# Two transformer blocks on one core: the first feed-forward matrix with 512-column matmuls, weights split three slabs ahead, and another rule for choosing weight buffers

## The reference, cut to what matters

```python
D_MODEL, SEQ, DEPTH, D_FF = 1024, 256, 2, 2816

def rmsnorm(x, g):
    y = xf * lax.rsqrt(jnp.mean(xf * xf, axis=-1, keepdims=True) + NORM_EPS)
    return y * g

def swiglu(x, w_in, w_out):                    # w_in 1024 x 5632, w_out 2816 x 1024
    a, b = jnp.split(x @ w_in, 2, axis=-1)
    return (jax.nn.silu(a) * b) @ w_out

for l in range(DEPTH):                         # first block; the second has the same frame
    x = x + 0.5 * swiglu(rmsnorm(x, ffn1_norm[l]), w_ffn1_in[l], w_ffn1_out[l])
    u = rmsnorm(x, mix_norm[l])
    ...                                        # u @ w_in[l], three branches, their gates
    x = x + merged @ w_out[l]
    x = x + 0.5 * swiglu(rmsnorm(x, ffn2_norm[l]), w_ffn2_in[l], w_ffn2_out[l])
```

## Time and profile before

| | |
|---|---|
| three timed executions, median | 3184.57 us |
| the profiled execution, device time | 3180.34 us |
| its span | 3178.6 us |
| TensorE busy in it | 2964.9 us (93%), 21202 matmuls |
| VectorE busy | 1693.3 us (53%) |
| ScalarE busy | 1389.1 us (44%) |
| granted TensorE clock, mean | 0.964 of full speed |
| DMA | 476.49 MB, mean 150 GB/s |

### The profile page before, as it was taken

The page is one execution under the profiler, slowest core; times in us unless marked ns, Lnnn a source line. Parts: engine busy times, 40 slices in busy tenths (PEclk is TensorE's granted clock), DMA queues, the critical chain, the costliest instruction groups (busy, mean ns, idle before and its releaser), DMA issues.

```text
span 3178.6 us, 49355 instructions
## 1 busy us (share of the span) xinstructions
PE 2964.9 (93%) x21202; PEld 2769.7 (87%) x21202; DVE 1693.3 (53%) x2846; ACT 1389.1 (44%) x1948; POOL 12.6 (0%) x20
## 2 busy tenths in 40 slices
PE   5998989999999899999999898899999999889997
PEld 5998778899998777799899896689989999667997
DVE  6656531566665842266665334456666643444665
ACT  4435442343444544244343345444444434544443
POOL 0000000000000000000000000000000000000000
PEclk9999999999999899999999899999999999899998
DMA  6543374555554242555464652355545565234552
GB/s 197 180 159 116 97 151 137 182 184 179 186 175 151 68 133 93 174 181 179 152 210 151 169 135 80 80 146 183 179 160 186 176 171 135 79 80 140 179 188 94
DMA packets 493544, 476.49 MB, mean 150 GB/s; under 512 B 63472, under 2 KB 476688, under 8 KB 493200
## 3 DMA queue, kind: packets, MB, share of 16 engines
q1 hardware_dynamic: 489744, 462.85, 47.0%
q0 software_dynamic: 3584, 10.49, 1.6%
HBM read 467.01 MB, written 6.29 MB: 149 GB/s over the span
## 4 chain that ended last, share of the span: by engine, by line
PE 87%; DVE 5%; ACT 4%; DMA 2%; issue 1%; SPq 0%; DVEq 0%; ACTq 0%
PE ps L781 36%; PE ps L852 31%; PE ps L872 16%; PE ps L954 2%; DVE WL L1539 1%; PE ps L812 1%; PE ps L929 1%; ACT REGION L1303 1%; DMA RAW<-in_w_o_mla 1%; DMA RAW<-in_w_in 1%; DMA RAW<-in_w_branch 0%; ACT REGION L1216 0%; ACT WH L1234 0%; ACT L1303 0%; ACT L1222 0%
## 5 line engine op out<-in xcount | busy, mean ns | idle before, releaser
L1539 DVE TENSOR_TENSOR WL<-RAW,WH 128x2048 fp32r<-128x2048 f32 (+1 forms) x342 | 761.4, 2234 | 476.8 <-ACT WH L1234 475.0
L1234 ACT ACTIVATE WH<-RAW 128x2048 fp32r<-128x2048 f32 (+1 forms) x342 | 633.2, 1858 | 238.5 <-DMA RAW<-in_ffn_wo 112.3
L781 PE MATMUL ps<-REGION,RAW 128*128 128x256 f32 (+3 forms) x1904 | 406.9, 376 | 65.1 <-DMA RAW<-in_w_o_mla 19.5
L781 PEld LDWEIGHTS ps<-REGION,RAW 128*128 128x128 f32 (+2 forms) x1904 | 346.7, 195 | 124.7 <-issue 50.5
L852 PE MATMUL ps<-UH,WH 128*128 128x256 f32 x2816 | 401.7, 285 | 29.8 <-ACT WH L1234 24.2
L852 PE MATMUL ps<-UH,WL 128*128 128x256 f32 x2816 | 395.1, 284 | 9.3 <-DVE WL L1539 9.3
L872 PE MATMUL ps<-HH,WH 128*128 128x256 f32 x1408 | 395.8, 281 | 2.4 <-DVE WL L1539 2.4
L872 PE MATMUL ps<-HH,WL 128*128 128x256 f32 x1408 | 396.1, 281 | 0.0
L872 PE MATMUL ps<-HL,WH 128*128 128x256 f32 x1408 | 395.5, 281 | 0.0
L852 PE MATMUL ps<-UL,WH 128*128 128x256 f32 x2816 | 394.2, 283 | 0.0
L852 PEld LDWEIGHTS ps<-UH,WH 128*128 128x128 f32 x2816 | 364.6, 192 | 33.9 <-issue 29.1
(11 more groups left out here) (212 smaller groups left out, 3067.0 us busy)
## 6 DMA issues: line engine op xcount, KB each, us to landing
RAW<-in_w_ffn_in SPq DMA_DIRECT2D x88, 1024.0 KB, 5.1
RAW<-in_ffn_wi SPq DMA_DIRECT2D x88, 1024.0 KB, 5.1
RAW<-in_w_in SPq DMA_DIRECT2D x86, 1024.0 KB, 5.5
RAW<-in_w_ffn_out SPq DMA_DIRECT2D x32, 1024.0 KB, 5.3
RAW<-in_ffn_wo SPq DMA_DIRECT2D x32, 1024.0 KB, 5.2
RAW<-in_w_out SPq DMA_DIRECT2D x16, 1024.0 KB, 8.8
RAW<-in_w_ffn_out SPq DMA_DIRECT2D x16, 768.0 KB, 4.4
RAW<-in_ffn_wo SPq DMA_DIRECT2D x16, 768.0 KB, 4.5
```

The lines of the kernel that those rows point to most:

```text
L781: last = nc.tensor.matmul(o, a, b, start=i == 0, stop=i == len(terms) - 1)
L1234: nc.scalar.activation(part_high(s), raw[pl.place[s]][:, 0:pl.words[s]], ACT.Copy).then_inc(weights_high, 1)
L1539: v_.tensor_tensor(part_low(s), raw[pl.place[s]][:, 0:pl.words[s]], part_high(s).bitcast(FP), ALU.subtract)\
```

## The change

Four edits, all in one:

1. `UH` and `UL` become two halves of one tile `UHL`, side by side for each feature tile. From slab 1 on, a product of the first matrix takes for each k one matmul with `WH` and 512 columns (UH and UL at once) and one with `WL` and 256 columns. The result stands in two halves of the bank: columns 0 to 255 hold WH·UH + WL·UH, columns 256 to 511 hold WH·UL.
2. The halves have to be added. For 42 of the 44 products ScalarE copies the second half to `TMP[:, side, T:2T]` (new function `tails`), VectorE waits for that copy (`tail_out`), adds it to the first half, and then multiplies by `RSTD` in a second instruction that waits for the first (`link`). Before, one multiplication did it.
3. The splits of the feed-forward part stand three slabs ahead (`AHEAD = 3`) where they stood two ahead.
4. `Plan.slab` takes the place that is free first by product number (`free_at`), the end of other use of `REGION` counted in, where it took the place with the oldest slab.

```diff
+AHEAD = 3
...
+    def free_at(self, p):
+        used = -1 if self.latest[p] is None else self.slab_last[self.latest[p]]
+        idle = -1 if self.idle_from[p] is None else self.idle_from[p]
+        return max(used, idle), -1 if self.latest[p] is None else self.latest[p], p
...
-        place = min(places, key=lambda p: (-1 if self.latest[p] is None else self.latest[p], p))
+        place = min(places, key=self.free_at)
...
-        UH, UL = sb("UH", [P, DK, T], FR), sb("UL", [P, DK, T], FR)
+        UHL = sb("UHL", [P, DK, 2, T], FR)
+        UH, UL = UHL[:, :, 0, :], UHL[:, :, 1, :]
...  # TensorE, ffn
+                        if j > 0:
+                            for k in range(DK):
+                                cols = slice(side * P, (side + 1) * P)
+                                both = (wh[:, k, cols], UHL[:, k, :, :], bank(n, 0, 2 * T))
+                                tail = (wl[:, k, cols], UH[:, k, :], bank(n, 0, T))
+                                for a, b, o in (both, tail) if k < DK - 1 else (tail, both):
+                                    last = nc.tensor.matmul(o, a, b, start=k == 0 and a is both[0], stop=k == DK - 1 and a is both[0])
+                            last.then_inc(product_done, 1)
+                            continue
...  # ScalarE, ffn
+                def tails(n):
+                    for side in range(2):
+                        wait_product(act, n + side)
+                        nc.scalar.activation(TMP[:, side, T:2 * T], bank(n + side, T, 2 * T), ACT.Copy).then_inc(tail_out, 1)
-                feed.to(s0 + 1)
+                feed.to(s0 + AHEAD - 1)
                 for j in range(FK // 2):
-                    feed.to(s0 + 2 * j + 2)
+                    feed.to(s0 + 2 * j + AHEAD)
                     if j == 0:
                         norm_x(first[name + ".norm"])
+                    else:
+                        for side in range(2):
+                            wait_evicted(act, n - 2 + side)
+                        tails(n)
                     for side in range(2):
                         wait_evicted(act, n + side)
                         nc.scalar.activation(SILU[:, side, :], SILU[:, side, :], ACT.Silu).then_inc(gate_done, 1)
-                    feed.to(s0 + 2 * j + 3)
+                    feed.to(s0 + 2 * j + AHEAD + 1)
+                    tails(p0 + 4 * j + 3)
                     hidden_parts(j)
...
-                            feed.to(s + len(PARTS) * q + t + 2)
+                            feed.to(min(s + len(PARTS) * q + t + AHEAD, s + len(PARTS) * DK // 2 - 1))
...  # VectorE, ffn (its feed.to lines change as ScalarE's do)
+                def scaled(dst, n, tail=None):
+                    if tail is not None:
+                        dve.wait_ge(tail_out, tally.add("tail_out") + 1)
+                        link(v_.tensor_tensor(dst, bank(n, 0, T), tail, ALU.add))
+                        v_.tensor_tensor(dst, dst, RSTD[:], ALU.mult).then_inc(evicted[n % BANKS], 1)
+                        return
-                        scaled(SILU[:, side, :], n + side)
+                        scaled(SILU[:, side, :], n + side, TMP[:, side, T:2 * T] if j > 0 else None)
-                    scaled(TMP[:, 0, 0:T], n)
-                    feed.to(s0 + 2 * j + 3)
-                    scaled(TMP[:, 1, 0:T], n + 1)
+                    scaled(TMP[:, 0, 0:T], n, TMP[:, 0, T:2 * T])
+                    feed.to(s0 + 2 * j + AHEAD + 1)
+                    scaled(TMP[:, 1, 0:T], n + 1, TMP[:, 1, T:2 * T])
```

More of the change, by code:

```diff
@@ L537, in build @@
         gate_done = sem("gate_done")
+        tail_out = sem("tail_out")
         ple_added = sem("ple_added")
@@ L1562, in ffn @@
                 hidden = tally.add("hidden", FK)
-                def scaled(dst, n):
+                def scaled(dst, n, tail=None):
[4 more added lines that the diff above has]
+                        return
                     wait_product(dve, n)
```

## The result

| | before | after |
|---|---|---|
| median of four runs, us | 3184.2 (3180.86 to 3188.91) | 3226.42 (3224.38 to 3237.09) |
| ratio | | 1.0138, 95% [1.0112, 1.0164] |
| span of the profiled execution, us | 3178.6 | 3223.2 |
| mean granted clock | 0.964 | 0.972 |

The account below looks back on a forecast made before the run. TensorE was taken as the bound, by 0.6 us in a pass of 11.4. 99 - 41 + 4.6 = +62 us on 3180.34 us gave 3243, and 3247 us for the median, range 3205 to 3300.

Parts of the forecast that it names:

- What bounds the kernel: First feed-forward matrix: TensorE bounds with 11.41 us a pass of two slabs, against 10.82 us for ScalarE and VectorE.
- Part 2, the pass: First feed-forward matrix: adding the halves lengthens the pass of ScalarE and VectorE by 2.45 us to 13.3 us.
- Part 3, the delay: Feed-forward parts, three slabs ahead: larger starting stock, yet each part 12.4 us later, +99 us for eight (+63 to +149).
- the ends of block 2's first parts: Last slabs of the second feed-forward matrix: -5.7 us in layer 0, +10.3 in layer 1, together +4.6 us.
- Part 1, the wide matmul: First feed-forward matrix: 512 columns take 218 ns, saving 53 us (0 to 66) if TensorE stayed the bound.
- Part 4, the places: Attention output and gate loads start earlier, so TensorE's waits for them go: -41 us (-30 to -43).
- The clock as a rival: First feed-forward matrix: the clock falls in TensorE's new gaps, +48 us, 3295 us; chance 0.09.
- The row of 1753 to 1754: Half-clock stretch: six 256-column matmuls and a seventh begun fit into 1 us, so 512 columns take at least 213 ns.
- TensorE stays the bound: First feed-forward matrix: ScalarE and VectorE keep up; 3095 us, or 3148 if 512 columns save nothing; chance 0.16 (0.10, 0.06).
- the 11.9 given as the point that decides: First feed-forward matrix: a pass of 11.9 us would mean no delay; under it TensorE stays the bound.
- The places don't help: Loads in the attentions: issued earlier, but a later slab is late instead; without the 41 us, 3288 us; chance 0.05.

Follow-up runs that it names:

- the places alone: Kernel before with nothing but the new rule for places (`free_at`): 3136.29 us, ratio 0.9851.
- the first two experiments: Kernel before with only the new rule for places: 3136.29 us; kernel after with the old rule for places: 3282.33 us.

## Why the prediction was right, and where its sizes were off

*What bounds the kernel.* Right. The 0.6 us between the pass and TensorE was the whole case, and it could not be seen from busy shares: VectorE is busy 57% of the span after the change and still sets the time of the first matrix.

*Part 2, the pass.* 13.3 us predicted, 13.28 measured; also 13.28 with the old places (VectorE's `a` additions at 641.56, 654.84 and 668.11). The middle split stood 3.00 us behind `WH`, as computed, and the copies for the `a` products were covered. The `TMP` addition waited for the copy and `WL` for `WH`. One reading was off: in a pass `WL` waits for ScalarE once, not twice, because the other wait is now the copy's. VectorE's busy time rose by 134.8 us (336 x 0.40; 0.42 predicted), ScalarE's by 96.1 us (336 x 0.29; 0.38 predicted). Two copies in a row overlap, 0.64 us for both at 622.05, where the single copy of the earlier trace rows takes 0.379.

*Part 3, the delay.* 12.4 us a part predicted, 145.1 - 133.1 = 12.0 measured. The additional split fitted into the wait ahead of the first scaling, as computed: 3.81 us before, 1.60 after. The eight parts with the ends were to cost 99 + 4.6 = 103.6 us and cost 103.4. To hit that so closely is in part luck. From first scaling to the next norm's matmul five parts grew by 12.1 to 12.3 us, some 97 us for eight, 2 less than the term. At the ends of block 2's first parts the sum holds: layer 0 grew 5.8 us less than the others and layer 1 10.3 us more (-5.7 and +10.3 predicted). But the first part of block 1's layer 1 grew by 14.0 us, 1.9 more than the others (1.8 of it with the places alone), and the prediction had nothing for it.

*Part 1, the wide matmul: the mis-sized term.* I took 218 ns for 512 columns, between 213 and 238. TensorE's timeline in the first slabs, each row the start of a matmul:

```profile
603.32 0.39 PE L861 MATMUL ps<-UHL,WH 128*128 128x512 f32 x1
603.55 0.27 PE L861 MATMUL ps<-UHL,WL 128*128 128x256 f32 x1
603.66 0.40 PE L861 MATMUL ps<-UHL,WH 128*128 128x512 f32 x1
```

512 columns take some 235 ns to the next start, 256 columns 117, the pair 0.35 us; 672 matmuls in 118.31 us say the same over a whole matrix (176 ns for each, so 352 for a pair). Nearly the upper bound. Twice the columns took twice the time, so what had kept 256 columns at 118 ns is no floor for each weight load, as I had argued from 30 columns at 114 ns, but looks like a rate by the column, 0.46 ns (two sizes were measured); that 30 columns of plain fp32 take as long must have another cause, which no run here isolates. The saving is 119.8 - 118.3 = 1.5 us a part, 12 us in all instead of 53, and without additions 15 us were measured. For the Trainium skill ("TensorE: Matmul & The Clock Gate", Back-to-back issue gap) the gap behind an isolated matmul of 512 columns comes to about 216 ns, and a sustained stream with weight loads needs about 131 ns for each; this kernel needed 235 for its kind of data, and the measurement decides. The error did not reach the forecast, since the pass and not TensorE set the time. It shows in one figure: TensorE has 11.27 us of work in a pass, not 10.8, and so lost (13.28 - 11.27) / 13.28 = 15% of each pass, not 20%. Its stock lasted longer for the same reason: it first waited at slab 12 (665.43), not at slab 10. It would have counted in the rival: with TensorE as the bound the time is 3121 us, halfway between the 3095 and 3148 given for it.

*Part 4, the places: right in kind, too small; the other mis-sized term.* -41 us predicted. TensorE's idle time in the mixing stages fell by 42.4 us, which is the term as worked out. But the stages were 61 to 62 us shorter in the kernel after, and 53 us shorter with the places alone. What I left out is the clock. The wait for `w_o_mla` in layer 0 of the kernel before ends at 479.54; the stretches around its end (us, busy PE, PEld, DVE, ACT, POOL with counts, clock, DMA share, GB/s):

```profile
475.00:480.00 5.00, 0.46 (x1) 0.49 (x2) 0.00 (x0) 0.00 (x0) 0.00 (x0) 0.50 1.05 363
480.00:485.00 5.00, 5.00 (x19) 4.13 (x18) 1.01 (x3) 0.00 (x0) 0.00 (x0) 0.74 0.72 241
485.00:490.00 5.00, 5.00 (x25) 4.41 (x24) 2.38 (x6) 0.00 (x0) 0.00 (x0) 1.00 0.15 40
```

So the matmuls behind the wait run at half speed for a while, and with the wait that goes too. Added up over the four mixing stages, TensorE is busy at the granted clock of 0.50 for 143.6 us before and for 104.9 us after. By the 213 and 118 ns of one matmul at the two levels, the 38.7 us between them are worth an estimated 17 us of the 19.7 us by which the busy time fell. Over the whole span the clock stands at 0.50 for 181 to 197 us in the seven kernels with the new rule and for 232 to 250 us in the three with the old one; that is one profile for each kernel. Between the forecast's 3243 us for the profiled execution and the 3224.94 measured lie 18 us: 20 from this term, less 2 in small ones. The other 2.6 us of the 20.6 are the distance from that execution to the median, 1.5 us after and 4.2 in the forecast.

*The clock as a rival.* Wrong. The stretch table of the kernel after, over the passes in which TensorE waits:

```profile
645.00:750.00 105.00, 95.36 (x564) 81.70 (x563) 71.69 (x114) 51.48 (x80) 0.00 (x0) 1.00 0.49 161
```

Gaps of 0.7 to 1.35 us, one in each pass of 13.28 us, left the granted clock at 1.00. The Trainium skill ("TensorE: Matmul & The Clock Gate", A second HAM failure mode) warns of repeated short idle times; the ones here did not bring the clock down. The longer gap of 3.87 us in the same kernel did (it ends at 2595.13), 0.72 on the mean of these 6 us:

```profile
2594.00:2600.00 6.00, 4.87 (x29) 4.87 (x29) 5.72 (x8) 1.91 (x1) 0.00 (x0) 0.72 1.24 232
```

*Two slips in the working.* The row of 1753 to 1754 counts six matmuls that lie in that microsecond at least in part; they start 0.213 us apart, so fewer than five fit into it, not six and a seventh begun. The lower bound of 213 ns comes from that distance and stands. And the range is not added up in one way: all lower bounds together give 3205 us, all upper ones 3313, while 3300 holds little more than the largest of them. The measured time lies inside either.

*The other rivals.* "TensorE stays the bound" had its point right: with a pass of 11.35 us (below the 11.9 given as the point that decides) the first matrix ran unbroken. "The places don't help" fell with the first two experiments.

## What to carry to other kernels

When two engines feed a third by turns, take the chain of one loop pass from their timelines and compare it with the third engine's time for the same pass; the busy shares hide it. Before paying for added work in such a chain, look whether one engine's part can be issued an iteration earlier: here the same additions cost 105 us in one order and nothing in the other. And judge an edit made of several by its halves: a gain of 48 us in the choice of buffers was buried under a loss of 90.

## What the runs showed that I had not expected

- At full clock an fp32r matmul of 512 columns took 235 ns and one of 256 some 117, so two matmuls with the same weights made into one save little: 1.5 us over the 336 pairs of one part, 4 ns each.
- The idle time shown ahead of a matmul understates a stall. At 664.33 a 512-column matmul starts; the next should start 0.235 us later, at 664.57, and starts at 665.43, which is 0.86 us late with 0.71 shown, since a matmul's busy time reaches past the start of its follower. Over the stretch from 602.80 to 750.20 TensorE shows 147.40 - 137.56 = 9.84 us of idle time, but the matmuls of it take 118.3 + 15.6 us unbroken, so 13.5 us were lost.
- Removing 42.4 us of idle time made the mixing stages 62.1 us shorter. Waits of several us cost more than their own length, since the matmuls behind them run at half clock; an estimated 17 us of the 19.7 us of busy time that went are that.
